# Six ring rows from the first gather on, and one weight chunk kept instead of loaded twice, in a two-layer decoder with product-key experts

## What is computed

```python
for i in range(DEPTH):                       # DEPTH = 2
    hn = rmsnorm(h, norm_mix[i])
    y = diff_attention(hn, ...) if i == 0 else short_conv(hn, ...)
    h = h + y
    h = h + peer_ffn(rmsnorm(h, norm_ffn[i]), peer_w_q[i], peer_keys[i], peer_u[i], peer_v[i])

def peer_ffn(h, w_q, sub_keys, u_tab, v_tab):   # in essence
    q = h @ w_q                                 # 1024 -> 2048
    s = q . sub_keys                            # 8 heads, 2 halves, 128 keys each
    idx, gates = top 16 of the 256 sums of the two halves' top 16, softmax over them
    act = gelu(u_tab[idx] . h) * gates          # 8 * 16 = 128 experts for each token
    return sum of act * v_tab[idx]
```

## Time and profile before

| | |
|---|---|
| median of 3 runs | 1521.54 us (1520.81 to 1522.27) |
| the profiled execution's own time | 1519.13 us |
| its span in the trace | 1517.3 us |
| PE busy | 1345.8 us, 89% |
| DVE busy | 991.8 us, 65% |
| ACT busy | 596.3 us, 39% |
| POOL busy | 578.3 us, 38% |
| bytes moved by DMA | 619.73 MB, of them 536.90 MB by the gathers |
| granted TensorE clock, mean | 0.988 |

### The profile page before, as it was taken

How to read it: one execution, slowest core, us unless ns; L and a number is a source line. 1 busy time by engine, 2 the same in 40 slices (tenths; PEclk the granted TensorE clock), 3 DMA queues, 4 the chain that set the end, 5 groups by cost and what they waited for, 6 DMA issues and landing times.

```text
span 1517.3 us, 12576 instructions
## 1 busy us (share of the span) xinstructions
PE 1345.8 (89%) x3294; PEld 572.1 (38%) x3294; DVE 991.8 (65%) x2412; ACT 596.3 (39%) x1805; POOL 578.3 (38%) x518
## 2 busy tenths in 40 slices
PE   9999899899878889999887899899989889777787
PEld 4444344344333333434332334344433333222222
DVE  4677877875656777546478546667567867764444
ACT  1334464643333433334334434244334344343333
POOL 0033334443323343445334444344433444444442
PEclk9999999999999899999999999999999999999999
DMA  9879999999999999999999999999999999999998
GB/s 389 344 290 421 364 425 419 421 413 421 422 422 425 417 420 413 401 418 420 422 419 403 420 417 401 422 421 420 417 421 417 413 415 420 412 413 421 421 421 335
DMA packets 85895, 619.73 MB, mean 408 GB/s; under 512 B 9536, under 2 KB 9664, under 8 KB 13760
## 3 DMA queue, kind: packets, MB, share of 16 engines
q0 software_dynamic: 74016, 536.90, 85.9%
q1 hardware_dynamic: 10080, 74.72, 12.0%
q10 hardware_dynamic: 1728, 7.31, 1.2%
HBM read 617.85 MB, written 1.05 MB: 408 GB/s over the span
## 4 chain that ended last, share of the span: by engine, by line
DMA 42%; PE 35%; DVE 13%; ACT 7%; issue 3%; SPq 0%; POOL 0%; DVEq 0%; POOLq 0%; ACTq 0%
DMA ring<-in_peer_uv_dram,idx 40%; PE acc L663 23%; PE pp L411 10%; DVE ring L1487 7%; ACT diag L1019 2%; DMA ring<-in_w_qkv_dram 2%; ACT weight L1015 1%; ACT L1013 1%; ACT gelu L1013 1%; ACT L875 1%; PE tt L426 1%; DVE top_i L1203 1%; DVE row_f L1248 0%; PE acc L411 0%; DVE pick L1245 0%
## 5 line engine op out<-in xcount | busy, mean ns | idle before, releaser
L663 PE MATMUL acc<-ring,diag 128*128 128x512 f32 x2048 | 994.7, 611 | 160.6 <-ACT diag L1019 154.4
L787 POOL DMA_INDIRECT ring<-in_peer_uv_dram,idx x510 | 574.1, 1126 | 922.3 <-PE acc L663 812.9
L1487 DVE CUSTOM_DVE_ANT_0 ring<-ring,xf 128x1024 f32<-128x1024 f32 x512 | 627.1, 1226 | 450.7 <-DMA ring<-in_peer_uv_dram,idx 437.3
L663 PEld LDWEIGHTS acc<-ring,diag 128*128 128x128 f32 x2048 | 370.9, 191 | 721.0 <-ACT diag L1019 374.4
L1013 ACT ACTIVATE gelu<-dots 128x1 f32<-128x1 f32 x512 | 103.6, 202 | 799.4 <-DVE dots L1487 796.9
L1019 ACT ACTIVATE diag<-const,weight 128x128 f32<-128x128 f32 x512 | 205.4, 401 | 16.8
L1015 ACT ACTIVATE weight<-gelu,gates 128x1 f32<-128x1 f32 x512 | 150.8, 295 | 16.6
L411 PE MATMUL pp<-stream,xT 128*128 128x512 f32 x160 | 80.6, 593 | 0.0
L411 PEld LDWEIGHTS pp<-stream,xT 128*128 128x128 f32 x160 | 29.9, 191 | 35.5 <-issue 35.5
L1487 DVE DVE_READ_ACCUMULATOR2_ANT dots<- 128x1 f32 x512 | 42.0, 82 | 0.0
L411 PE MATMUL pp<-stream,xf 128*128 128x512 f32 x80 | 40.9, 592 | 0.0
(11 more groups left out here) (164 smaller groups left out, 764.6 us busy)
## 6 DMA issues: line engine op xcount, KB each, us to landing
stream<-in_peer_w_q_dram SPq DMA_DIRECT2D x18, 1024.0 KB
stream<-in_conv_w_in_dram SPq DMA_DIRECT2D x8, 1024.0 KB
ring<-in_peer_uv_dram,idx POOLq DMA_INDIRECT x510, 10.3
stream<-in_w_qkv_dram SPq DMA_DIRECT2D x4, 1024.0 KB
ring<-in_w_qkv_dram SPq DMA_DIRECT2D x2, 2048.0 KB, 26.7
stream<-in_w_o_dram SPq DMA_DIRECT2D x4, 1024.0 KB
kept<-in_peer_w_q_dram SPq DMA_DIRECT2D x2, 2048.0 KB
ring<-in_w_qkv_dram SPq DMA_DIRECT2D x2, 1024.0 KB, 11.4
```

What stands on the lines that cost most here:

```text
L663: mm = nc.tensor.matmul(acc[half][:, :], diag[:, s % RING, :], row[:, D + half * 512:D + (half + 1) * 512], start=(k == 0), stop=(k == SLO ...
L787: nc.gpsimd.indirect_dma_start(dst, None, uv_dram, bass.IndirectOffsetOnAxis(idx[:, at:at + 1], 0)).then_inc(landed, 16)
L1487: nc.vector.tensor_tensor_reduce(row[:, 0:D], row[:, 0:D], xf[:, s // SLOTS % 2, :], 1.0, 0.0, ALU.mult, ALU.add, dots[:, s % RING:s % RIN ...
```

## The change

`RING` stays 8, but the gathers of all 512 slots go round six rows, in the order 6, 7, 4, 5, 0, 1. Rows 2 and 3 (place 3) keep the first layer's input chunk 3 from the front part on; the second block's projection reads it there, and its second load into `STREAM` is gone. When that projection is done, the second layer's input chunk 5 is loaded into place 3; place 10 and its wait for `v_used` are gone. The order of all other loads in the list stays. `first_junk` is now the tile `pick`, which has the same size.

```diff
-SHARED = {(1, "in", 0), (1, "in", 4), (1, "in", 5), (1, "out", 0), (1, "wq", 3),
+SHARED = {(1, "in", 0), (1, "in", 3), (1, "in", 4), (1, "in", 5), (1, "out", 0), (1, "wq", 3),
...
-        w_in = {place: sem(f"w_in{place}") for place in range(2, 11)}
+        w_in = {place: sem(f"w_in{place}") for place in range(2, 10)}
...
-        places = {STREAM: stream[:, :], 6: spare[:, :], 7: kept[:, 0, :], 8: kept[:, 1, :], 9: kept_work, 10: ring[:, 6:8, :].rearrange("p r d -> p (r d)")}
+        places = {STREAM: stream[:, :], 6: spare[:, :], 7: kept[:, 0, :], 8: kept[:, 1, :], 9: kept_work}
...
-        loads += [(0, "wq", 2, STREAM), (1, "in", 3, STREAM), (0, "wq", 3, 7),
+        loads += [(0, "wq", 2, STREAM), (0, "wq", 3, 7),
                   (1, "out", 1, STREAM), (1, "wq", 0, STREAM), (1, "wq", 1, STREAM), (1, "wq", 2, STREAM)]
-        loads += [(2, "in", 2, 6), (2, "out", 0, 8), (2, "in", 4, STREAM), (2, "in", 3, 7), (2, "out", 1, 9), (2, "in", 5, 10), (2, "in", 0, STREAM),
+        loads += [(2, "in", 2, 6), (2, "out", 0, 8), (2, "in", 4, STREAM), (2, "in", 3, 7), (2, "out", 1, 9), (2, "in", 5, 3), (2, "in", 0, STREAM),
...
-        FIRST_ROWS, LATER_ROWS = (2, 3, 6, 7, 4, 5, 0, 1), (2, 3, 4, 5, 0, 1)
-        row_of = [FIRST_ROWS[s % RING] if s < SLOTS else LATER_ROWS[(s - SLOTS) % len(LATER_ROWS)] for s in range(ALL)]
+        ROWS = (6, 7, 4, 5, 0, 1)
+        row_of = [ROWS[s % len(ROWS)] for s in range(ALL)]
...
-                    elif place == 10:
-                        sp.wait_ge(v_used, max(s for s in range(ALL) if row_of[s] in (6, 7)) + 1)
...
-                    if s < RING:
+                    if row_before[s] is None:
                         if ring_at(s) < 2:
                             written(pool, ff, (1, "in", 4))
-                        elif ring_at(s) < 4:
-                            written(pool, pp, (0, "in", 3))
                         elif ring_at(s) < 6:
...
-            first_junk = ring[:, 2, 0:D]
+            first_junk = pick[:, :, :].rearrange("p j c -> p (j c)")
```

## The result

| | before | after |
|---|---|---|
| median | 1521.17 us (1520.39 to 1522.27, 4 runs) | 1530.64 us (1529.68 to 1531.30, 4 runs) |
| span of the profiled execution | 1517.3 us | 1528.5 us |

The account below looks back on a forecast made before the run. PE was taken to bound the full-ring stretches and DMA the rest; the two stretches' shifts, 2λ − 6.5 with λ at 6.0, gave +5.5 us on the median 1521.54: 1527.0 us, 0.36% slower, range 1520.0 to 1531.2.

Parts of the forecast that it names:

- What bounds the kernel: PE sets the pace where the ring fills, chiefly 164 to 196 us; DMA where weights load or side steps are missing.
- The load that goes: 2 MB less on SP's queue at 186.11 us: −5.0 us of DMA work, if the engines are kept busy.
- The front part: First gathers on their new rows, and sums of squares written elsewhere: no cost.
- First stretch, Δ1 = λ − 4.2: Full ring at slots 25 to 45: slot 43 lands later, shifting slot 62 by λ − 4.2 us, saved load included.
- λ: Time a gather takes from issue to landing when nothing stands before it: taken as 6.0 us, between 3.4 and 8.1.
- The lump: 4 MB of loads together at 220 us: slots 45 to 48 one to two us later, nothing added by slot 62.
- Second stretch, Δ2 = λ − 2.3: Full ring at slots 64 to 80: a further delay of λ − 2.3 us, not given back later.
- 2λ − 6.5: Sum of both stretches' shifts: +5.5 us at 6.0, +0.4 at 3.4, +9.7 at 8.1.
- A: Rival, both full stretches: a gather's delay is short, 3.4 us, giving +0.4, 1521.9 us; chance 0.15.
- B: Rival: only the first stretch counts and the second's delay vanishes, giving +1.8, 1523.3 us; chance 0.12.
- C: Rival, decided at 196 to 220 us by 422 GB/s: six rows suffice, −5.0 us, 1516.5; chance 0.12.
- D: Rival, slots 31 to 77: DVE loses its lead, PE waits 3.7 us more, 1530.7; sign: new `diag` waits before 240; chance 0.13.

Follow-up runs that it names:

- e2_less_load: Kernel before, eight rows, with only 16 of 2048 columns brought of each part of input chunk 3's second load: 1520.40 us, ratio 1.0002.
- e3_spread: Changed kernel with the two parts of the second block's output chunk held back until v_used 43 and 47: 1530.14 us, ratio 1.0066.
- e6_six_late: Kernel before, with eight rows for slots 0 to 55 and six from slot 56 on: 1525.50 us, ratio 1.0036.
- e5_six_even: Kernel before with its loads kept, all slots going round six rows in one even order: 1531.98 us, ratio 1.0081.
- e7_seven_rows: Kernel before, with seven rows for slots 0 to 127: 1525.88 us, ratio 1.0032.
- e4_rejoin: Changed kernel, with rows 2 and 3 joining the ring so that slots 52 to 127 go round eight rows: 1526.88 us, ratio 1.0037.
- e8_swap: Changed kernel, six rows, with the second block's output chunk loaded before query chunk 3: 1529.18 us, ratio 1.0048.
- e1_six_rows: Kernel before with its loads kept, slots 0 to 127 on six rows in an order that doesn't join the later one: 1534.31 us, ratio 1.0096.

## Why the prediction was right, and where it was off

**What bounds the kernel.** Right. PE's times up to slot 43 are the same in both kernels (+0.1 us), the DMA rate falls where the ring is full, and from slot 95 on the two run in parallel up to slot 127, and later but for what the clock adds.

**The load that goes, −5.0 us "if the engines are kept busy".** They are not: alone it is worth nothing (e2_less_load). Leaving it out of the gain was right.

**The front part.** Nothing, as said: +0.1 us at slot 43 holds it all.

**First stretch, Δ1 = λ − 4.2.** The form was right for the gather it is about: slot 43 was issued at 216.66, took 8.03 us, and landed at 224.70, 3.97 us late. But the shift at slot 62 was 5.4. The landings' lateness goes from 3.97 to 5.4 us between slots 43 and 52, and the step that did not hold is the DMA work "without a gap in both kernels" from 220 us on: 391 GB/s at 220 to 232 against 423 are 0.4 MB, 0.9 us. The rest is not settled. In this execution PE's waits at slots 44 to 47 were followed by a halved clock (granted 0.79 over 244 to 252, 1.00 before), but e3_spread, without the lump and with a clock of 1.00 there, ended the stretch at 4.8.

**The lump.** Its worth was right, nothing (e3_spread). How late slots 45 to 48 would land was not: one to two microseconds were forecast, and they landed 7.4 to 9.8 us late, 5.1 to 7.3 in e3_spread.

**Second stretch, Δ2 = λ − 2.3.** It gives 5.5 with the 7.80 us of slot 78; measured 10.6 − 5.4 = 5.2, and 5.3 by itself in e6_six_late.

**λ, the term that was mis-sized.** I took 6.0 from one gather at 172.66 us as the case of the full stretch. It was issued when the engines came out of a pause (share 0.57 over 170 to 172). The two sums are about gathers at the end of a full stretch, and these took 8.03 and 7.80 us. In the changed kernel the gathers issued from 164 to 187 us took 6.1 to 7.0 us, those from 188 to 217 took 7.4 to 9.1. A steady pace alone does not make the difference: in e2_less_load the gathers of slots 34 to 37 go out 2.6 to 3.0 us apart and take 5.5 to 5.9; it is 7.5 only from slot 40 on. From slot 34 to 43 they are issued every 2.73 us and land every 2.96, and the lag adds up. Why each takes 2.96 us there and not 2.49 is open; the last section has what the packets show.

The value was to be had: slot 78's own gather, in the second full stretch before, took 8.4. Also my upper bound, 8.1, fits, which I had laid aside because I thought a queue stood behind it; it is what kept the measured time inside the range. 2λ − 6.5 with 8.0 gives +9.5 us, where 9.5 were measured; so near a fit is luck, as the traces give 10.6 at slot 95.

The rule of the Trainium skill (DMA: Bandwidth & Descriptors, the anatomy of one DMA), an estimate of 4.4 us for a gather, would have given +2.3; the traces don't agree with it, their shortest gather being 5.4 us. The same page of the Trainium skill has a table of measured transfers (section on bandwidth) with 6.15 us for 1 MB. It counts only the time in which the DMA engines are busy, so it is not the same thing as issue to landing, which was 6.0 in the earlier trace rows and 8.0 here.

**The rivals.** A falls with λ at 8.0 in place of 3.4, and B with the second step, which e6_six_late shows alone. C was to be decided at 196 to 220: 378 GB/s, not 422. It falls, and e2_less_load adds that even eight rows don't let the bytes through. D, in part: PE's waits for `diag` from 164 to 344 us rose from 7.3 to 14.9 us, the longest staying at 3.7. The new ones begin at slot 44, with 0.47 us up to 235.39 and 2.17 up to 240.40, behind late gathers. By the letter that is the prediction's own sign for D, new waits ahead of 240. DVE's waits for landings rose from 21.8 to 34.3 us in the same stretch; whether its shorter lead has a share of its own was not tested.

## What to carry to other kernels

The worth of a prefetch ring is read in the stretches where the consumer sets the pace: each row is one slot of lead in each such stretch that fills the ring, here 2.5 to 3 us, and it is worth something only if a transfer-bound stretch follows, as here behind slots 43 and 80. Bytes saved where the consumer sets the pace and the ring is full are worth nothing. The DMA rate before does not warn of it: it was 422 GB/s with the load in that stretch and 356 without. When sizing such a ring, take a transfer's latency from the gathers that the sum is about, here those at the end of a full stretch (8 us), not from one early in it (6 us).

## What the runs showed of the hardware

A DMA share near 1 doesn't mean full rate. From the packet records of the traces, the gathers' 8 KB packets from 196 to 220 us:

```
                packets   over 500 ns   mean of these   median of all
before             1105        2             657 ns         312 ns
after              1105       50 (4.5%)      878 ns         309 ns
e2_less_load       1040       71 (6.8%)      867 ns         309 ns
```

When the queues are kept deep nearly every packet takes 312 ns; when the ring holds them shallow, one in twenty takes almost three times as long and still counts as busy. That goes with the 98% share at 378 GB/s: 50 packets with 0.57 us more each are 1.8 us of each of 16 engines, 7% of the 24 us. That these are the first packets of an engine that had run dry was not shown; the records don't name the engine.

The other was PE's clock. In 890 to 905 us the granted clock was 1.00 before and in the changed kernel, but not in e5_six_even:

```profile
890.00:905.00 15.00, 11.49 (x21) 4.73 (x20) 5.01 (x10) 4.19 (x15) 2.82 (x3) 0.77 1.01 421
```

In e6_six_late and e7_seven_rows it was 0.89 there. PE's shift grew between slots 250 and 300 by 2.7 us in those two, by 4.6 in e4_rejoin and e8_swap and by 6 in e5_six_even, but not in the changed kernel, though nothing near those slots differed; it fell back only in part. In e5_six_even 2.9 of the 6 us came at once with the lower clock at 897 us. So a small shift in time can move where the clock halves, and single traces differ at their end by some microseconds that are not the edit's. The shifts at slot 95 to 127, ahead of that, are the cleaner measure here, but not a sharp one: the 12.3 and 9.2 us of e1_six_rows and e5_six_even are the same program up to there.
